# Where an activation tile begins in its partition: a two-layer block on one Trainium2 core

## What is computed

```python
def first_block(x, c, ...):            # cut
    mod = (silu(c) @ w_ada + b_ada)    # shifts, scales, gates
    hn = modulate(rmsnorm(x, norm1_g), shift1, scale1)
    proj = hn @ w_in                   # q, k, v of two attentions, gates
    ya = dsa_attention(...); yb = stick_breaking_attention(...)
    merged = sigmoid(ga) * (ya @ w_proj_a) + sigmoid(gb) * (yb @ w_proj_b)
    x = x + gate1 * (merged @ w_out)
    hn2 = modulate(rmsnorm(x, norm2_g), shift2, scale2)
    f = peer_ffn(hn2, w_q, sub_keys, u, v)   # 16384 experts, top 16 of 8 heads
    x = x + gate2 * f
    return rmsnorm(x, final_g)

def second_block(x, mem, ...):         # cut
    x = x + hybrid_mixer(rmsnorm(x), ...)            # conv, MoBA, GLA
    x = x + memory_cross_attention(rmsnorm(x), rmsnorm(mem), ...)
    x = x + conv_ffn(rmsnorm(x), w_up, conv_w, conv_b, w_down)
    return rmsnorm(x)
```

## The kernel before, in words

| tile | first byte, before | past a multiple of 256 | after | past a multiple of 256 |
|---|---|---|---|---|
| ringb | 16,512 | 128 | 16,512 | 128 |
| split (3 buffers) | 32,896 | 128 | 32,896 | 128 |
| xT | 57,472 | 128 | 57,472 | 128 |
| H (H_all) | 65,856 | 64 | 66,304 | 0 |
| Hf, in H_all | 65,920 | 128 | 66,432 | 128 |
| cst | 82,304 | 128 | 82,816 | 128 |
| rT | 87,296 | 0 | 87,360 | 64 |
| far, PR, far2 | 92,416 | 0 | 92,480 | 64 |
| PA | 104,704 | 0 | 104,768 | 64 |
| Yb, Ya | 187,200, 195,392 | 64 | the same | 64 |
| split1 | 212,864 | 128 | the same | 128 |
| cpw, rt | 223,488, 226,048 | 0 | 223,552, 226,112 | 64 |
| Ym, MH, act_t | 117,056, 133,440, 117,056 | 64 | the same | 64 |
| split4, split5 | 162,176, 219,520 | 128 | the same | 128 |

## Time and profile before

### The profile page before, as it was taken

The page is one execution under the profiler, slowest core; times in us unless marked ns, Lnnn a source line. Parts: engine busy times, 40 slices in busy tenths (PEclk is TensorE's granted clock), DMA queues, the critical chain, the costliest instruction groups (busy, mean ns, idle before and its releaser), DMA issues.

```text
span 1438.1 us, 25879 instructions
## 1 busy us (share of the span) xinstructions
PE 1390.4 (97%) x10406; PEld 1292.4 (90%) x10406; DVE 1095.1 (76%) x1903; ACT 836.4 (58%) x1447; POOL 359.6 (25%) x227
## 2 busy tenths in 40 slices
PE   7999999899999999999999999999999999899997
PEld 5988899899999999999988888887889899799997
DVE  7788897567889888999766666677667667798862
ACT  4554774444454687777654454565446666776651
POOL 3216201234445100000032322344322321433200
PEclk9999999999999999999999999999999999999999
DMA  9768775556665454444566666665667636276630
GB/s 387 273 200 266 250 247 170 164 156 184 189 185 161 153 156 148 147 148 147 151 189 221 195 192 195 212 198 178 197 191 254 195 115 193 75 248 191 196 113 30
DMA packets 73721, 268.24 MB, mean 187 GB/s; under 512 B 8401, under 2 KB 9730, under 8 KB 72834
## 3 DMA queue, kind: packets, MB, share of 16 engines
q1 hardware_dynamic: 71280, 256.41, 56.1%
q10 hardware_dynamic: 1426, 7.56, 1.5%
q0 software_dynamic: 896, 2.62, 0.5%
HBM read 262.88 MB, written 3.67 MB: 185 GB/s over the span
## 4 chain that ended last, share of the span: by engine, by line
PE 80%; DVE 13%; ACT 4%; POOL 1%; DMA 1%; issue 1%; DVEq 0%; ACTq 0%; POOLq 0%
PE bank L611 79%; DVE split L1834 3%; DVE ada_acc L1869 2%; DVE PR L2284 1%; DVE PR L2281 1%; DMA ringb<-in_w_ada 1%; POOL H L2652 1%; ACT split L1298 1%; DVE PR L2289 1%; PE bank L787 0%; DVE rT L1920 0%; POOL split L2625 0%; DVE H L2373 0%; DMA vecs<-in_vecs 0%; DVE PA L2085 0%
## 5 line engine op out<-in xcount | busy, mean ns | idle before, releaser
L611 PE MATMUL bank<-H,split 128*128 128x256 f32 x5928 | 724.8, 283 | 17.9 <-DVE split L1834 6.8
L611 PEld LDWEIGHTS bank<-H,split 128*128 128x128 f32 x5928 | 703.1, 191 | 24.7 <-issue 9.4
L1298 ACT CAST split<-ringb 128x1024 fp32r<-128x1024 f32 x350 | 365.9, 1047 | 284.8 <-PE bank L611 270.4
L2625 POOL TENSOR_TENSOR split<-ringb,split 128x1024 fp32r<-128x1024 f32 x91 | 226.7, 2491 | 665.6 <-ACT split L1298 665.6
L611 PE MATMUL bank<-split,H 128*128 128x512 f32 (+1 forms) x1728 | 390.5, 387 | 1.5 <-POOL split L2625 1.5
L1834 DVE TENSOR_TENSOR split<-ringb,split 128x1024 fp32r<-128x1024 f32 x259 | 326.0, 1262 | 74.9 <-ACT split L1298 74.8
L611 PEld LDWEIGHTS bank<-split,H 128*128 128x128 f32 x1728 | 320.9, 188 | 69.1 <-POOL split L2625 2.5
L2373 DVE TENSOR_TENSOR H<-PR,H 128x256 fp32r<-128x256 f32 x128 | 137.3, 1073 | 106.4 <-ACT H L1637 106.4
L1298 ACT CAST split<-far 128x1024 fp32r<-128x1024 f32 x89 | 93.1, 1048 | 53.4 <-PE bank L611 43.1
L1834 DVE TENSOR_TENSOR split<-far,split 128x1024 fp32r<-128x1024 f32 x77 | 99.7, 1304 | 31.5 <-ACT split L1298 31.3
L1613 ACT ACTIVATE PR<-bank 128x512 f32<-128x512 f32 (+31 forms) x59 | 28.7, 487 | 74.5 <-PE bank L611 74.5
(11 more groups left out here) (298 smaller groups left out, 1264.4 us busy)
## 6 DMA issues: line engine op xcount, KB each, us to landing
ringb<-in_u SPq DMA_DIRECT2D x128, 512.0 KB, 3.8
ringb<-in_v SPq DMA_DIRECT2D x128, 512.0 KB, 4.4
ringb<-in_w_ada SPq DMA_DIRECT2D x28, 512.0 KB, 5.4
far<-in_w_up SPq DMA_DIRECT2D x26, 512.0 KB, 4.3
far<-in_w_ada SPq DMA_DIRECT2D x20, 512.0 KB, 5.2
ringb<-in_w_up SPq DMA_DIRECT2D x17, 512.0 KB, 4.7
ringb<-in_w_pq SPq DMA_DIRECT2D x16, 512.0 KB, 4.2
far<-in_w_dn SPq DMA_DIRECT2D x14, 512.0 KB, 4.2
```

The source lines that it names most:

```text
L611: return TE.matmul(o, l, r, start=start, stop=stop, skip_group_check=True)
L1298: S.copy(buf(m)[0], slots[P.slot[m]]).then_inc(hi_done, 1)
L2625: G.tensor_tensor(lo, slots[P.slot[m]], hi.bitcast(F32), ALU.subtract).then_inc(lo_g, 1)
```

## The change

H_all is declared behind `sm` (160 elements) and not behind `mod` (48 elements), and `mod` goes to the place of `sm`. H_all grows by 16 elements, and Hf begins 32 elements into it and not 16. PA gives up 16 elements, and the spacers gap1 and gap3 (16 elements each) go. Each instruction, wait and queue keeps its place on its engine; line numbers below L408 fall by one and below L416 by two.

```diff
@@ -376,13 +376,13 @@
         xT = sb("xT", [128, 8, T])
-        mod = sb("mod", [128, 48])
-
-        H_all = sb("H", [128, 16 + 16 * T], F32R)
+        sm = sb("sm", [128, 160])
+
+        H_all = sb("H", [128, 32 + 16 * T], F32R)
         H = H_all[:, 0:16 * T].rearrange("p (z k t) -> p z k t", z=2, k=8)
         cst = sb("cst", [128, 768])
         vecs = sb("vecs", [128, A["vecs"].shape[1]])
-        sm = sb("sm", [128, 160])
+        mod = sb("mod", [128, 48])
@@ -390,7 +390,7 @@
             far = sb("far", [128, 3, UNIT], where=ph)
-            PA = sb("PA", [128, 20624], where=ph)
+            PA = sb("PA", [128, 20608], where=ph)
@@ -405,7 +405,6 @@
         far2 = sb("far2", [128, 6, UNIT])
         with ExitStack() as ph:
-            sb("gap1", [128, 16], where=ph)
             Ym = sb("Ym", [128, 2, 8, T], F32R, where=ph)
@@ -413,7 +412,6 @@
         with ExitStack() as ph:
-            sb("gap3", [128, 16], where=ph)
             act_t = sb("act_t", [128, 2, 22, T], F32R, where=ph)
@@ -469,7 +467,7 @@
-        Hf = H_all[:, 16:16 + 16 * T]
+        Hf = H_all[:, 32:32 + 16 * T]
```

## The result

The changed kernel takes 1458.97 us (median of 4 runs, 1452.4 to 1462.53), against 1437.72 before on the same chip: ratio 1.0136, 95% interval 1.0095 to 1.0177. Forecast was 1446, with a range up to 1453. A second set, with new runs of the kernel before beside it, gave 1454.11 (1453.22 to 1456.36) against 1441.23: 1.0095, interval 1.0071 to 1.0118. So it is slower by 1.0 to 1.4%, 13 to 21 us; the side was right, the size was not. The first set's four times, 1462.53, 1459.26, 1458.69 and 1452.4 us, stand in the order of their mean granted clocks, 0.986, 0.989, 0.991 and 0.993, so part of its spread comes with the clock and not with the tiles. And 1437.72 is low for the kernel before: four later sets, 54 runs in all, have medians from 1438.6 to 1441.2.

The account below looks back on a forecast made before the run. PE's matmuls, their count times the step from start to start, were taken to bound the kernel. H's move added 9 us and the other edits 0, so 1437.2 + 9 = 1446 us, range 1425 to 1453.

Parts of the forecast that it names:

- That a product's cadence sets the time: Whole kernel: time is the matmul count times the step from one start to the next, 113.3 or 117.9 ns for H.
- Edits 2 to 4: Hf's offset, tiles keeping their addresses, and moved rT, far, PR, `mod`, `sm`: 0, bounds -1 to +1 us.
- The distance between moving tile and weights: H products: pace depends on the two tiles' addresses modulo 256; H's distance goes from 64 to 128.
- the failed step: H products: quick stretches mostly turn slow, a third of the loss won back; 2,850 x 4.5 ns x 0.7 = 9 us.
- all slow: Upper bound on H products: every quick one falls to 117.9 ns, 2,850 x 4.5 = 13 us.
- rival C: H products pay another 4.5 ns beyond slow, 122 ns: 1477 us, or about 1460 with half the stages; chance 8%.
- The reason for the direction: One step of 64 from a settled distance costs wide products at least 2.2 ns; H products move one such step.
- Rival A: Distance acts modulo 128, so H's slow products turn quick as in the v stage: -9 us, 1428; chance 28%.
- Rival B: Pace is set by how the stream starts after a break: 1437 within 2 us; 14% with address rounding.
- The rule told beside it: TensorE has independent read ports for moving operand and weights, so the two addresses could not matter: no change in time.

Follow-up runs that it names:

- others_64: Changed kernel with H left 64 bytes past a multiple of 256 and `mod` and `sm` unmoved; 1439.66 us, 1.0001 of the kernel before.
- all_192: Kernel before with a 192-byte spacer in front of every tile, so all places move and all distances stay; 1439.99 us, ratio 1.0009.
- the table: Matmul-only kernel, 8 x 8 places of moving tile and weights 32 bytes apart: 120.0 ns at distance 0, 117.8 at +64, 113.3 or 117.8 at -64.
- The second profile: Changed kernel run and profiled once more, nothing altered; 1454.11 us against 1441.23 before, ratio 1.0095.
- the small kernel: Whole computation left out but for matmuls, two tiles filled once and placed at chosen bytes; 113.3 ns a product at the quickest places with 256 columns.
- h240: Kernel before with H moved to 240 bytes past a multiple of 256 (112 beyond the weights), Hf still at 128; 1430.74 us, ratio 0.9945.
- the small kernel of the finer steps: Matmuls only, weights at 128, moving tile at 64 places 4 bytes apart, four starts; all four reached 113.3 ns only at 240.

## Why the prediction was right or wrong

*That a product's cadence sets the time, and that only addresses change:* right. 19.6 of PE's 23.3 us more are H products, and PE's idle time didn't grow.

*Edits 2 to 4 at nothing:* right. `v` kept 226.7 ns, Ya its 11.04 us, and others_64 lies at 1.0001; its interval, 3 us either way, is wider than the stated bound of 1 us.

*The distance between moving tile and weights, not the tile's own place:* right, and shown by all_192 and by the table's diagonals.

*The size, the failed step:* "I take it that the quick stretches lose their pace, most of them to the slow value, with a third of the loss won back in stretches that are slow now". Two things in it were wrong; the share of quick products was not, since 2,834 of the 5,602 H steps at full clock before are under 116 ns. I took the two cadences seen, 113.3 and 117.9 ns, for the only ones that a distance can have. They belong to -64; in the whole kernel 128 has its own, 118.7 and 120.0, both above. So the slow products paid too (long stretch: 117.9 to 118.8 ns; a slow unit of `u`: 3.07 to 3.12 us), and the quick ones paid 6.7 in `w_up`, not 4.5. And nothing was won back. By the steps from start to start at full clock (those under 135 ns), the mean went from 115.6 to 119.3 ns, so the term is 5,928 x 3.7 ns = 22 us in place of 9. The steps above, nearly all at half clock, took 2.4 us less than before (210 of them, then 200), which leaves about the 19.6 of the group's 744.4 less 724.8. The second profile's mean of 119.0 gives 20 to 21 us. The bound of 13 us for "all slow" was no bound, for the same reason, and the range of 1453 rested on it; rival C, a third and dearer pace at 8%, was nearest: its 122 ns was too high, but its form for half of the stages came to 1460. What sets 120.0 in one run and 118.7 in the other, at one distance, stays open.

*The reason for the direction* didn't hold, and that the side came out right was luck as far as this reason goes. The step of 64 from distance 0 in the wide products did cost, and a step from -64 costs here; but the table shows no rule of steps. The sign was also left out: the value projections lie at +64 and the H products at -64, and with 256 columns the two aren't alike (117.8 ns against 113.3 or 117.8). What holds is that 113.3 ns is rare: of 64 places three have it at all, so that most moves away from one of them cost.

*Rival A* had its sign from the wide products. At distance 0 they have their floor, and narrow ones 120.0 ns. *Rival B's* reason, that the start of a stream sets the pace, holds between the two values of one distance and not between distances. The rule told beside it, that PE's two reads of SBUF have independent ports and never wait (the Trainium skill, SBUF — State Buffer, on the two separate sides), is contradicted here for 4-byte elements: the small kernel has 113.3 to over 123 ns by the place of one tile. For bfloat16 the runs agree with it to 0.8 ns. Of the other page's estimate of 109.2 ns (the Trainium skill, TensorE: Matmul & The Clock Gate, on 56 ns against 53.3 ns) the same holds: bfloat16 runs at just that, and float32r never settled below 113.3.

*A slip without effect:* DVE's idle share is 24% by its 76% busy, not the 28% written; no term hung on it.

*The median:* the before itself ran from 1429.67 to 1447.65 us in one set of 17 runs, which three runs within 1.1 us had hidden. A stretch at -64 may go either way, so one profile's shares of quick and slow were a draw: of the 63 whole units of `u`, 22 were quick before, 42 in others_64 and all 63 in all_192. That isn't the whole spread: in those 17 runs the slower ones mostly had the lower mean granted clock, down to 0.987 from 0.992.

## What to carry to other kernels

In a kernel bound by float32r matmuls, compare the steps from start to start between stretches of one form before looking for waits; if they differ at full clock, look at where the moving tile and the stationary one begin modulo 256. Measure the few places with a small kernel that has nothing but the matmuls, each from several starts, and take one at which all starts settle low (here moving minus weights = +112 for 256 columns; for 512 it was 0, from one start in each small kernel and throughout `v`). Do it for each width apart. In bfloat16 it was worth under 1 ns a product here. When a resource shows two values at one setting, another setting may have other values: they are no bounds.

## What the runs showed that I had not expected

- Four bytes are enough: 113.3 ns at 240, 121.8 or more at 244.
- One program at one distance has two lasting cadences (113.3 and 117.8 at -64, 118.7 and 120.0 at 128), chosen at a restart and kept over up to a thousand products; act_t's 528 took 60.3 or 62.3 us from run to run in h240.
- With 512 moving columns, the weights' tile moving and at 128, 226.7 ns came only with the stationary tile at 128, 112 and 248, of 32 places tried 8 bytes apart in the small kernel of the finer steps; most others gave 233.3.
